# A hybrid decoder layer with 64 routed experts: a wider slot table, earlier counts, a reordered pair of copies and one wait less

## What is computed

```
u = RMSNorm(x);  [B|C|h|q|k|v] = u @ W_in
y_c = B * causal_dwconv3(C * h)
y_a = sliding-window attention (window 128, QK-norm, ALiBi, sinks)
x = x + concat(RMSNorm(y_c), RMSNorm(y_a)) @ W_out
xn = RMSNorm(x)
scores = sigmoid(xn @ W_router)        # 64 experts, 8 groups, best 4 groups, top 8
w = scores of the chosen 8, normalised, * 2.5
x = x + sum over chosen e of w[e] * SwiGLU_e(xn) + SwiGLU_shared(xn)
```

## Time and profile before

| | before |
|---|---|
| median of three runs | 1532.47 us |
| the profiled execution | 1534.66 us |
| its span in the profile | 1532.9 us |
| PE busy | 1481.9 us, 97% |
| DVE, ACT, POOL busy | 671.2, 298.9, 688.9 us |
| share of the final chain | PE 88%, DMA 5%, DVE 2% |
| DMA moved | 328.93 MB, mean 215 GB/s |

### The profile page before, as it was taken

How to read it: one execution, slowest core, us unless ns; L and a number is a source line. 1 busy time by engine, 2 the same in 40 slices (tenths; PEclk the granted TensorE clock), 3 DMA queues, 4 the chain that set the end, 5 groups by cost and what they waited for, 6 DMA issues and landing times.

```text
span 1532.9 us, 24188 instructions
## 1 busy us (share of the span) xinstructions
PE 1481.9 (97%) x6703; PEld 658.8 (43%) x6704; DVE 671.2 (44%) x886; ACT 298.9 (19%) x567; POOL 688.9 (45%) x638
## 2 busy tenths in 40 slices
PE   7999999999999869999999999999999999999995
PEld 3556556556555433333333333333333333333332
DVE  1444354354353524444444444444444444444441
ACT  1223323323332101111111111111111111111110
POOL 2010212212230414665665666566656656665661
PEclk9999999999998989999999999999999999999998
DMA  9411211211185629989899989787899998998936
GB/s 348 150 51 50 76 42 36 76 42 35 63 322 66 162 91 350 301 260 333 266 349 275 336 255 286 239 264 248 277 336 346 294 312 265 298 306 248 326 40 167
DMA packets 74571, 328.93 MB, mean 215 GB/s; under 512 B 15161, under 2 KB 16698, under 8 KB 48806
## 3 DMA queue, kind: packets, MB, share of 16 engines
q1 hardware_dynamic: 44438, 248.01, 44.8%
q0 software_dynamic: 30096, 80.45, 22.3%
HBM read 284.31 MB, written 65.08 MB: 228 GB/s over the span
## 4 chain that ended last, share of the span: by engine, by line
PE 88%; DMA 5%; DVE 2%; issue 2%; POOL 1%; ACT 0%; another core or an unknown queue 0%; SPq 0%; POOLq 0%; DVEq 0%; ACTq 0%
PE psP L692 51%; PE psW L692 29%; PE psT L845 5%; DMA xnT_dram<-area 1%; DMA wts<-in_w_in_dram 1%; PE psW L907 1%; DMA area<-x_dram 1%; DMA slot_table<-pay,slot_i 1%; PE psW L743 1%; POOL slot_table L587 0%; PE psT L700 0%; PE psT L779 0%; DVE area L1386 0%; ACT L1117 0%
## 5 line engine op out<-in xcount | busy, mean ns | idle before, releaser
L692 PE MATMUL psP<-wts,bias 128*64 (+1 forms) x1296 | 575.9, 597 | 3.5 <-issue 3.5
L692 PE MATMUL psP<-area,bias 128*64 128x512 f32 x1264 | 561.0, 597 | 0.0
L692 PE MATMUL psW<-wts,area 128*64 (+2 forms) x1592 | 429.1, 594 | 6.4 <-DVE wts L1560 2.0
L692 PEld LDWEIGHTS psP<-wts,bias 128*64 128x64 f32 (+1 forms) x1296 | 172.7, 138 | 339.5 <-issue 339.5
L692 PE MATMUL psP<-wts,area 128*128 128x512 f32 (+1 forms) x704 | 288.8, 562 | 6.1 <-DMA wts<-in_w_in_dram 4.7
L692 PEld LDWEIGHTS psW<-wts,area 128*64 128x64 f32 (+1 forms) x1592 | 150.6, 148 | 258.2 <-issue 250.4
L651 POOL DMA_INDIRECT out_dram<-area,sidx x79 | 123.4, 1562 | 264.6 <-ACT area L1182 129.2
L1552 DVE COPY area<-wts 128x4096 f32 x81 | 186.0, 2296 | 97.0 <-issue 87.7
L632 POOL COPY gidx<-area 128x1 int32 (+1 forms) x83 | 203.1, 2447 | 25.6 <-PE psT L845 21.5
L1518 DVE COPY bias<-psT 128x1024 f32<-128x1024 f32 x81 | 99.1, 1224 | 246.8 <-PE psT L845 243.6
L692 PEld LDWEIGHTS psP<-wts,area 128*128 128x128 f32 x704 | 131.9, 192 | 137.8 <-issue 128.1
(11 more groups left out here) (214 smaller groups left out, 821.7 us busy)
## 6 DMA issues: line engine op xcount, KB each, us to landing
wts<-in_w_exp_gate_dram SPq DMA_DIRECT2D x64, 1024.0 KB
wts<-in_w_exp_up_dram SPq DMA_DIRECT2D x64, 1024.0 KB
wts<-in_w_exp_down_dram SPq DMA_DIRECT2D x64, 1024.0 KB, 7.3
wts<-in_w_in_dram SPq DMA_DIRECT2D x4, 2048.0 KB, 17.6
area<-in_x_dram SPq DMA_DIRECT2D x8, 512.0 KB, 3.4
wts<-in_w_out_dram SPq DMA_DIRECT2D x1, 4096.0 KB, 18.3
area<-u_dram SPq DMA_DIRECT2D x16, 256.0 KB, 2.8
xn_dram<-area POOLq DMA_DIRECT2D x8, 512.0 KB
```

Source lines behind the costliest of these rows:

```text
L692: return nc.tensor.matmul(out_, lhsT, rhs, start=start, stop=stop)
```

## The change

Five edits. The rows of the slot table are ROW = S + HB = 1088 places apart (8704 bytes) in place of 1024. A second row of `eo_bf`, partition 32, adds 64 per expert to the base; the first fill of the table is 544 KB in pieces of 1088 bytes; the gather's row numbers use 17 rows of 64 per expert. TensorE loads its two loop counts in the middle of `gate_up(5)` and the job count `n` after the loop. `gate_up_late(0)` does four of its eight steps ahead of the last `down_halves`, not two. In the loop of VectorE `copy_dn(r)` stands ahead of `read_xT`. GpSimd no longer waits for `s_merged` at its end.

```diff
+    ROW = S + HB
-        table = nc.dram_tensor("slot_table", [NE * S, 2], F32).ap()
+        table = nc.dram_tensor("slot_table", [NE * ROW, 2], F32).ap()
...
-    CD = 13
+    CD = 14
...
-        def routed_jobs(eng, c, jobs):
+        def routed_jobs(eng, c, jobs, counts=None):
...
-            pairs = eng.value_load(n_jobs[0:1, 2 + c:3 + c], min_val=MIN_JOBS // 2 - c, max_val=JMAX // 2)
-            full = eng.value_load(n_jobs[0:1, 4 + c:5 + c], min_val=MIN_JOBS // 4 - c, max_val=JMAX // 4)
+            pairs, full = counts or pair_counts(eng, c)     # pair_counts: the same two loads
...
-            sp.dma_start(table.rearrange("(p q j) c -> p q (j c)", p=P, q=NE * S // (P * P)),
-                         bc(tabT[:, 0:P, :]...
+            width = NE * ROW // (4 * P)
+            sp.dma_start(table.rearrange("(p q j) c -> p q (j c)", p=P, q=4),
+                         bc(tabT[:, 0:width, :]...
...
-            pool.wait_ge(s_merged, 16 * NSH * P // rows)
...
-            gate_up(5)
+            gate_up(5, range(0, 3))
+            pe.wait_ge(s_n_jobs, 4)
+            counts = pair_counts(pe, 0)
+            gate_up(5, range(3, KT))
...
-            pe.wait_ge(s_n_jobs, 4)
-            n = pe.value_load(n_jobs[0:1, 0:1], min_val=MIN_JOBS, max_val=JMAX)
...
-            routed_jobs(pe, 0, jobs)
+            routed_jobs(pe, 0, jobs, counts)
+            n = pe.value_load(n_jobs[0:1, 0:1], min_val=MIN_JOBS, max_val=JMAX)
             last = pe.value_load(ring_i[0:1, bass.ds(n, 1)], min_val=0, max_val=NE)
-            gate_up_late(0, range(0, 2))
+            gate_up_late(0, range(0, 4))
             down_halves(n + (NSH - 1), (last % NSLOT) * SLOTW)
-            gate_up_late(0, range(2, KT))
+            gate_up_late(0, range(4, KT))
...
+                V.tensor_scalar(eo_bf[32:33, :], eo_i[32:33, :], float(ROW - S) / S, None, ALU.mult)
...
-                                       scalar=float(S // HB), in1=iota_p[0:JMAX, b:b + 1], op0=ALU.mult,
+                                       scalar=float(ROW // HB), in1=iota_p[0:JMAX, b:b + 1], op0=ALU.mult,
...
                     h_mul(r + NSH, k, tab_w[:, bass.ds(r, 1)])
+                    copy_dn(r)
                     read_xT(r + (NSH + 2), k)
-                    copy_dn(r)
                     copy_gu(r + 2, k)
```

More of the change, by code:

```diff
@@ L325, in shared_place, with pair_counts @@
             return xT_shared[j], r_ld[j]
-        def routed_jobs(eng, c, jobs):
-            pairs = eng.value_load(n_jobs[0:1, 2 + c:3 + c], min_val=MIN_JOBS // 2 - c, max_val=JMAX // 2)
-            full = eng.value_load(n_jobs[0:1, 4 + c:5 + c], min_val=MIN_JOBS // 4 - c, max_val=JMAX // 4)
+        def pair_counts(eng, c):
+            return (eng.value_load(n_jobs[0:1, 2 + c:3 + c], min_val=MIN_JOBS // 2 - c, max_val=JMAX // 2),
+                    eng.value_load(n_jobs[0:1, 4 + c:5 + c], min_val=MIN_JOBS // 4 - c, max_val=JMAX // 4))
+        def routed_jobs(eng, c, jobs, counts=None):
+            pairs, full = counts or pair_counts(eng, c)
             with eng.Fori(0, full) as i:
@@ L372, in _ @@
             sp.wait_ge(s_const_dve, 5)
-            sp.dma_start(table.rearrange("(p q j) c -> p q (j c)", p=P, q=NE * S // (P * P)),
-                         bc(tabT[:, 0:P, :].rearrange("p j c -> p (j c)").unsqueeze(1), [P, NE * S // (P * P), 2 * P])) \
+            width = NE * ROW // (4 * P)
+            sp.dma_start(table.rearrange("(p q j) c -> p q (j c)", p=P, q=4),
+                         bc(tabT[:, 0:width, :].rearrange("p j c -> p (j c)").unsqueeze(1), [P, 4, 2 * width])) \
               .then_inc(s_init_st, 16)
@@ L625, in _ @@
                                         in_offset=bass.IndirectOffsetOnAxis(ap=jobrow_i[:, b:b + 1], axis=0),
-                                        bounds_check=NE * S // HB - 1, oob_is_err=False).then_inc(s_jobs_ld, 16)
+                                        bounds_check=NE * ROW // HB - 1, oob_is_err=False).then_inc(s_jobs_ld, 16)
             def gather(j, par, copies):
@@ L1251, in constants @@
                 V.tensor_copy(eo_bf[0:1, :], eo_i[0:1, :]).then_inc(s_const_dve, 1)
+                V.tensor_scalar(eo_bf[32:33, :], eo_i[32:33, :], float(ROW - S) / S, None, ALU.mult) \
+                 .then_inc(s_const_dve, 1)
                 V.tensor_scalar(iota_p[:, 0:1], tok_i[:, 0, 0:1], 2.0, None, ALU.mult).then_inc(s_const_dve, 1)
```

## The result

| | before | after |
|---|---|---|
| median | 1534.11 us (5 runs, 1530.87 to 1535.72) | 1519.21 us (5 runs, 1513.37 to 1521.19) |
| the profiled execution | 1534.66 us | 1521.13 us |
| its span in the profile | 1532.9 us | 1519.4 us |

The account below looks back on a forecast made before the run. The prediction took TensorE to bound the loop (busy 924.86 of 925 us), with gains in the handover, tail and block end. Its terms, 9.46 + 1.11 + 2.2 + 0.9 + 2.0 + 0.8 + 5.0 = 21.5 us, gave 1511.0 us; range 1508 to 1526.

Parts of the forecast that it names:

- The bound and the pitch: TensorE bounds the loop, busy 924.86 of 925 us; at the handover, rows 8192 bytes apart jam the scatters' writes in memory.
- GpSimd did not become the bound: Rival in the loop: moved copies block GpSimd until it bounds the loop, 1549 us or 1535 with the pitch; 6%.
- The first rival: At the handover: the pitch is not the cause, the jam stays, 7.8 us are left, 1524.7 us; 27%.
- my picture of the addresses: Slot table: pending writes stand at nearly the same offset in every row; 8704 bytes spread them over 32 KB of offsets.
- The table's wait: Handover: TensorE's wait for the gathered table vanishes in full, 9.46 us.
- The clock behind it: Handover: without the idling, eight matmuls and three transposes behind the table's wait run at the higher clock, 2.2 us.
- The first job: Loop start: the gap before it shrinks, so half of 1.76 us of lower clock returns, 0.9 us.
- Counts: Loop entry: three loads moved off the gap before the loop gain 2.0 us, hidden at their new places.
- The store of xnT: Ahead of the handover: a store at 458 us, delayed by the same jam, no longer holds TensorE, 1.11 us.
- The tail: End: the down copy ahead of the read of x brings the weight copy and GpSimd's last add forward, 0.8 us.
- The DRAIN: Block end: without the wait for the merges, GpSimd's DRAIN of 5.997 us runs earlier and overlaps, 5.0 us.
- The rival I gave 18% in all: Block end: the DRAIN waits for DMAs in flight, no 5.0 us; 1516.0 us with the pitch (11%), 1529.7 without (7%).

Follow-up runs that it names:

- q8: The changed kernel with slot table rows 2048 entries (16384 bytes) apart instead of 1088: 1528.22 us, ratio 0.993 to the kernel before.
- q6: The changed kernel with VectorE's first weight copy moved behind the reading of the gathered table: 1531.34 us, ratio 0.993 to the kernel before.
- q10: The changed kernel with VectorE's first weight copy behind the read of shared tile 3 and SyncE's store and load held until the table is gathered: 1524.07 us, ratio 0.990.
- p3: The changed kernel with GpSimd's wait for the merges at its end put back: 1526.19 us, ratio 0.992 to the kernel before.
- a1_after: The changed kernel itself, unaltered, run again on another chip: 1508.17 us, ratio 0.981 to the kernel before.
- q7: The changed kernel with slot table rows 1536 entries (12288 bytes) apart instead of 1088: 1526.16 us, ratio 0.992 to the kernel before.
- p5: The changed kernel with TensorE's three count loads put back between the last token transposes and the loop: 1513.32 us, ratio 0.984 to the kernel before.
- p2: The changed kernel with the old pitch, rows 1024 entries apart: 1535.73 us, ratio 0.997 to the kernel before.
- p4: The changed kernel with the read of x put back ahead of the down copy in VectorE's loop: 1509.65 us, ratio 0.982 to the kernel before.
- b1: The kernel before, unaltered, run once more on a third chip: 1539.85 us.

## Why the prediction was right, and where its steps failed

**The bound and the pitch: right.** The loop did not move: TensorE is busy for all of the 912 us from 562 to 1474, with 11.69 us a job as before. GpSimd did not become the bound, though its adds got 1.0 us longer. By the Trainium skill ("DMA: Bandwidth & Descriptors", section "Latency and other measured facts") plain copies keep their speed at a row pitch of 512 KiB, and a pad of 192 bytes did not heal one of 4 MiB. Carried over to a pitch of 8 KiB and scatters of eight bytes, that does not hold: 512 bytes more took the last landing from 13.01 to 4.30 us. The first rival, with 27%, is out. But my picture of the addresses, places that meet at the same offset in every row, failed too (`q8`): that the pitch is the cause is shown, what it does in memory is not.

**The table's wait: 7.4 us, not 9.46.** I let the scatters land in 2.54 us and GpSimd's part stay as it was, 4.67 us. They landed in 4.30 (2.1 to 3.1 in the eight other profiles with this pitch), and GpSimd's part grew to 5.96 us. VectorE copies weights at 529.63 us in before and at 529.87 in after; before, GpSimd still waited for its scatters then, and now its first gather falls just on that copy. Before, then after:

```profile
529.63 2.29 DVE L1552 COPY area<-wts 128x4096 f32 x1 [0.32 <-issue]
```

```profile
529.88 2.44 POOL L629 DMA_INDIRECT tabT<-slot_table,jobrow_i  x1 [4.19 <-DMA slot_table<-pay,slot_i]
```

```profile
529.87 2.33 DVE L1561 COPY area<-wts 128x4096 f32 x1 [0.33 <-issue]
```

1.04 us of issue became 2.44, and up to 3.70 in other profiles; with the copy moved away it is 1.04 again (`q6`, `q10`). I knew this lock, had cited it for the tail ("SBUF — State Buffer", section "SBUF: two separate sides", of the Trainium skill; the rows agree), and did not ask what GpSimd would meet at its new time.

**The clock behind it: 0.9 us, not 2.2.** The term hung on the wait going to zero. With 2.06 us left, the eight matmuls still took 5.00 us in after, though 3.60 in `p3` with 2.05; where 1.05 or 0.80 us were left (`a1_after`, `q10`), 3.60.

**The first job: 1.7 us, not 0.9.** I took half for a gap that shrinks; it came back whole. A half was no outcome that a row had shown: behind a gap of 1.33 us the job took 7.09 us, behind 3.45 it took 9.25. Nor is the gap all: `q7` and `q8` had gaps of 1.28 and 1.26 us and needed 10.0, with a wait of 2.9 and 3.5 us for the table some 16 us earlier, and `q6` needed 8.78 behind 1.30.

**Counts: right** (2.13 for 2.0), and free where they went. What I had not seen is that this edit carries the first job's clock: `p5` puts both together at 5.1 us.

**The store of xnT: -0.3 us for 1.11.** The wait is gone, and the mechanism was right, but beside it TensorE had run at its lower clock already in before (`p_v` in 5.01 us), which hid most of the jam; in after it ran slower still and ate the rest. My bounds, 0 and 1.11, were those of one profile. Where the clock holds, the term is 7.1 us and the 2.4 of the projection behind it (`p3` against `p2`), and the clock there is 6.6 of the 13.2 us by which the span of `a1_after` is below that of after. The five runs of after also fall into 1513 to 1514 and 1519 to 1521 us, some 6.6 us apart, as 18.39 and 11.83 are; that these are the two clocks is argued, not shown. How much of this term a run shows is luck, and the forecast had no place for it.

**The tail: 0.1 us, not 0.8.** TensorE lost its wait of 2.01 us (in `p4`, with the old order, 0.30 is left: the four steps of `gate_up_late` cover most of it), and it was right that this alone brings nothing. From `gate_up_late(0)` to the last add pass 12.34 us in before and `p4` and 12.21 in after and `a1_after`: the order is worth the 0.13. But I followed only the index copy, 2.72 us before. Of after's tail, GpSimd and VectorE:

```profile
1478.19 3.32 POOL L657 DMA_INDIRECT x_dram<-area,sidx  x1 [0.30 <-issue]
1481.02 0.69 POOL L638 COPY gidx<-area 128x1 int32 x1
...
1486.85 1.41 POOL L657 DMA_INDIRECT x_dram<-area,sidx  x1 [0.30 <-issue]
```

```profile
1475.32 1.23 DVE L1569 COPY wts<-wts 128x2048 f32 x1 [3.77 <-issue]
...
1477.93 2.29 DVE L1561 COPY area<-wts 128x4096 f32 x1 [0.26 <-issue]
```

The copy of 2.72 us is 0.69 now, but the add ahead of it is held in its place, 3.32 us: in both orders the weight copy catches one of them.

**The DRAIN: 1.2 us, not 5.0.** The rival I gave 18% in all was right. My argument against it, that the 5.997 us came after everything had landed, showed only that a DRAIN costs that with nothing in flight. It said nothing on whether it can run while something is.

So the sign was right, and the largest term was the one I had put first. The sum was 8 us too large in the profile: 3.5 of it the DRAIN by the stretches, 2.0 the table, 1.4 the store, 1.3 the clock behind the table, 0.7 the tail; the first job and the counts gave 0.9 more than forecast. That the time stayed in the range is in part luck. The range was kept wide for the case that the pitch does nothing, and what filled it was the DRAIN and a sum of smaller misses, while a gain in the front that the sum did not hold can be had or lost with the clock.

## What to carry to other kernels

Where a stall is taken out, list what every other engine will be doing at the new time, and price the next one to be late by the row of that collision, not by the row of a quiet moment. A wait on TensorE has a second price in the clock of the work behind it, so that two gaps taken out together can be worth more than the sum of each alone, and a saving can be hidden in one profile and open in the next. Before a step is counted as overlapped, look for a row in which it did run beside the work that is to cover it.

## What was not expected of the hardware

- Eight-byte scatters to rows 8192 bytes apart land 10 to 13 us after the last is issued, and a plain store beside them takes 21.6 and 24.3 us (before, `b1`); at 8704, 12288 and 16384 bytes they land in 2.1 to 4.3 us.
- GpSimd's DRAIN waits for the DMAs that GpSimd has issued, then needs 4.9 us more; with nothing in flight it takes 5.7 to 6.0 us, SyncE's 0.013.
- After 1.77 to 1.95 us of idling ahead of `p_v` TensorE fell to its lower clock in six profiles (1.83: `p_v` in 6.79 us) and not in four (1.93: 3.79 us), and the four had not idled less; after 0.25 us it fell in none of four.
